# Down stage of a streaming encoder step: ScalarE's norm work of a finished chunk moved later in its order

## The chip, the cores and the metric

The kernel runs on one core of a Trainium2 chip. The metric is the device time of one execution in microseconds. Before the change the median of three runs is 1325.32 us (1324.27 to 1325.89).

## The reference

One layer of a hybrid encoder on 1024 prompt frames and 64 sample frames (1088 tokens, width 1024, all fp32):

```
h = modulate(rmsnorm(x)); mix of retention and window attention; x = x + g1 * (mix @ w_out)
h2 = modulate(rmsnorm(x))
a, b = split(h2 @ w_up);  y = (silu(causal_conv(a)) * b) @ w_down        # D_FF = 2816
x = x + g2 * y
out = rmsnorm(x) * (1 + scale_f) + shift_f                                # final norm, adaLN
```

scale_f and shift_f come from silu(c) @ w_ada_f + b_ada_f. The change touches the last three lines alone: the down projection and the final norm.

## The kernel before, in words

Everything is transposed: features lie on partitions, tokens along the free axis. fp32 products are made from two parts: each weight tile is split into a rounded high half (ScalarE, a copy to fp32r) and the rest (GpSimd, a subtraction), and each output takes three matmuls (high x high, high x low, low x high).

The down stage runs 3 token chunks (364, 362, 362 tokens) x 22 row tiles of w_down = 66 steps, numbered q = 22 c + f with q from 0 to 65. A step multiplies one 128-row tile of the weights with the matching tile of u for eight output tiles o, each with its own PSUM bank: 24 matmuls. Each chunk reads all 22 weight tiles again.

- SP's queue (from L692) issues, at its index q, u tile q + 6 (load_u, L655) and weight tile q + 6 (load_down, L646). Weight tiles land in a ring of three raw buffers, so load q waits until GpSimd has split tile q - 3. The u tiles have a ring of eight, so u tile q waits until TensorE has ended step q - 8. In the same order stand the residual tiles of x (L676), the 16 loads of the last modulation weights (load_last_ada, L678, each waiting for VectorE's dots two tiles earlier) and the stores of finished chunks (store_y, L683).
- ScalarE (from L1171) at index q makes the high half of weight tile q (down_hi, L1092) and writes it into a ring of ten split tiles (w_more 4, w_hl 3, w_extra 3). Between the splits stand, written out by hand, the work of the chunk that is done: eight squares (final_square, L1142), the root of the mean (final_root, L1151) and eight modulations (final_modulate, L1157).
- GpSimd (down_lo, L1312) makes the low halves in order.
- VectorE: the dots of the last modulation weights, tiles 0 to 8 (last_ada_dots, L1832: two halves each, prompt and sample), then for each chunk eight evictions with the residual added (down_out, L1807), eight norm adds (final_add, L1817: a copy and seven adds into acc), the reciprocal (L1845); for chunk 0 dots 9 to 15; then eight scalings (final_scale, L1847).
- TensorE (from L2235): in the first four steps of chunks 1 and 2 it leaves out output tile 7, as bank 7 holds the norm's sum over partitions (final_sum, L2206), which it multiplies after step f = 2; after f = 3 it waits for the root and makes tile 7 of the four steps. The last four steps of chunk 2 run output tile by output tile.

ScalarE's squares use a ring of two buffers, so a square waits for VectorE's add two squares earlier, and the first of them waits for the first eviction. The order of every engine is fixed in the text: an engine that waits for one instruction holds all behind it.

Of the kernel before, what the change touches and what calls it, by code (L numbers as in the profile page):

```python
# [37 lines left out]
FT = D_FF // P  # L38
# [40 lines left out]
            [(CHUNKS[i][0], sum(CHUNKS[i])) for i in c]] + [(k, 0, T) for k in range(2, KT - 1)]  # L79
           + [(KT - 1, a, a + n) for a, n in CHUNKS])  # L80
LATE = 4

OUT_JOBS = ([(o, n) for o in range(1, 8) for n in (0, 1)] + [(o, n) for o in (4, 5, 3, 7) for n in (2, 3)]
            + [(o, n) for n in (2, 3) for o in (6, 1, 2)])
# [27 lines left out]
def hymba_step(nc, x_t, w_units, w_ada, b_ada, cond, gains, conv_wb, conv_st, sinks, ck_t, cv_in, st_in,  # L112
# [4 lines left out]
    with ExitStack() as ctx:  # L117
# [254 lines left out]
        def pieces(c):  # L372

            a, n = CHUNKS[c]
            if c < 2:
                return [(0, a, n, 0)]
            return [(0, a, C2P, 0), (C2P, S_PROMPT, S_SAMPLE, 1)]
# [118 lines left out]
        def _(sp):  # L496
# [149 lines left out]
            def load_down(q):  # L646
                c, f = divmod(q, FT)
                if q < 3:
                    sp.wait_ge(bl_ready, PRODUCTS * FT)
                else:  # L650
                    sp.wait_ge(dl_ready, q - 3 + 1)
                sp.dma_start(w_raw[:, q % 3], w_units[down_unit(f)].rearrange("p (k m) -> p k m", k=KT)).then_inc(
                    dw_loaded[q % 3], 16)

            def load_u(q):  # L655
                c, f = divmod(q, FT)
                a, n = CHUNKS[c]
                if q < U_RING:
                    sp.wait_ge(product, 2 * PRODUCTS * FT - PRODUCTS)
                else:  # L660
                    sp.wait_ge(down_step, q - U_RING + 1)
                if c == 0:
                    sp.wait_ge(u_hi_stored, 16 * (f + 1))
                    sp.wait_ge(u_lo_stored, 16 * (f + 1))
                sp.dma_start(u_hl[:, q % U_RING, :, 0:n].bitcast(F32), u_dram[f, :, :, a:a + n].rearrange("w p t -> p w t")).then_inc(
                    du_loaded[q % U_RING], 16)

            def load_residual(c):
                a, n = CHUNKS[c]
                sp.wait_ge(x1_stored[0], 32)  # L670
                sp.wait_ge(x1_stored[1], 80)
                sp.wait_ge(x1_stored[2], 32)
                sp.wait_ge(product, 2 * PRODUCTS * FT)
                sp.wait_ge(u_ready, FT)
                sp.wait_ge(ext_ready, FT)
                sp.dma_start(x_res[:, :, a:a + n], x1_dram[:, :, a:a + n]).then_inc(x1_again[c], 16)  # L676

            def load_last_ada(t):  # L678
                if t >= 2:
                    sp.wait_ge(ada_d_used, 2 * (t - 2) + 2)  # L680
                sp.dma_start(ada_d[:, t % 2], w_ada[48 + t]).then_inc(ada_d_loaded[t % 2], 16)

            def store_y(c, k0, k1, by_act, by_dve):  # L683
                a, n = CHUNKS[c]
                sp.wait_ge(y_by_act, by_act)
                if by_dve:
                    sp.wait_ge(y_seq, by_dve)
                sp.dma_start(y_v[:, k0:k1, a:a + n], x_res[:, k0:k1, a:a + n]).then_inc(stored, 16)
# [10 lines left out]
            for q in range(3 * FT):  # L699
                c, f = divmod(q, FT)  # L700
                if q == 1:
                    sp.dma_start(silu_d[:, :, :], cond.partition_broadcast(P)).then_inc(cond_again, 16)
                if 2 <= q < 34 and q % 2 == 0:
                    load_last_ada((q - 2) // 2)
                if q + 6 < 3 * FT:
                    load_u(q + 6)
                    load_down(q + 6)
                if q in (8, 26, 46):
                    load_residual(c)
                if c == 1 and f == 20 or c == 2 and f == 12:  # L710
                    store_y(c - 1, 0, 4, 8 * c - 4, 0)
                    store_y(c - 1, 4, 8, 8 * c, 0)
            store_y(2, 0, 2, 19, 0)
            store_y(2, 5, 6, 19, 2)
            store_y(2, 2, 5, 21, 2)
# [6 lines left out]
        def _(act):  # L722
# [357 lines left out]
            def silu(f):  # L1080
                act.wait_ge(conv_seq, 3 * f + 3)
                act.activation(conv[:, :], conv[:, :], ACT.Silu).then_inc(silu_ready, 1)

            def u_hi(f):

                act.wait_ge(u_ready, f + 1)
                if f > 0:
                    act.wait_ge(u_hi_stored, 16 * f)
                    act.wait_ge(u_lo_made, f)
                act.activation(acc[:, :].bitcast(F32R), up_b[f % 2][:, :], ACT.Copy).then_inc(u_hi_made, 1)  # L1090

            def down_hi(q):  # L1092

                act.wait_ge(dw_loaded[q % 3], 16 * (q // 3 + 1))
                if q < W_MORE:
                    act.wait_ge(product, 2 * PRODUCTS * FT - PRODUCTS)
                elif q < W_RING:
                    act.wait_ge(product, 2 * PRODUCTS * FT)
                    if q >= W_MORE + 3:
                        act.wait_ge(u_lo_stored, 16 * FT)  # L1100
                else:
                    act.wait_ge(down_step, q - W_RING + 1)
                act.activation(w_down(q)[:, 0], w_raw[:, q % 3], ACT.Copy).then_inc(dh_ready, 1)  # L1103
# [38 lines left out]
            def final_square(c, k):  # L1142

                a, n = CHUNKS[c]
                item = 8 * c + k
                act.wait_ge(down_evac, item + 1)
                if item >= 2:
                    act.wait_ge(fsq_used, item - 1)
                act.activation(sq[:, k % 2, 0:n], x_res[:, k, a:a + n], ACT.Square).then_inc(fsq_ready, 1)

            def final_root(c):  # L1151
                n = CHUNKS[c][1]
                act.wait_ge(fsum_ready, c + 1)
                act.activation(std[:, c, 0:n], bank[7 if c < 2 else 0][:, 0:n], ACT.Sqrt, bias=eps_sb[:, 0:1],
                               scale=1.0 / D).then_inc(fstd_ready, 1)

            def final_modulate(c, k):  # L1157

                if c == 2 and k in FINAL_POOL:
                    act.wait_ge(scaled_pool, FINAL_POOL.index(k) + 1)  # L1160
                elif c == 2:
                    act.wait_ge(scaled_dve, 17 + k - len(FINAL_POOL))
                else:
                    act.wait_ge(scaled_dve, 8 * c + k + 1)
                for o, tok, m, part in pieces(c):
                    y = x_res[:, k, tok:tok + m]
                    ins = act.activation(y, y, ACT.Identity, bias=mod[:, 48 + 2 * k + 1, part:part + 1],
                                         scale=scale_n[:, 2, k, part:part + 1])
                ins.then_inc(y_by_act, 1)

            for q in range(3 * FT):  # L1171
                c, f = divmod(q, FT)
                if q > 2:
                    down_hi(q)
                if q == 3:
                    silu(FT - 1)
                    u_hi(FT - 1)
                if q == 6:
                    act.wait_ge(cond_again, 16)
                    act.activation(silu_d[:, :, :], silu_d[:, :, :], ACT.Silu).then_inc(silu_d_ready, 1)  # L1180
                if c > 0:
                    if f < 2:
                        for k in range(4 * f, 4 * f + 4):
                            final_square(c - 1, k)
                    if f == 3:
                        final_root(c - 1)
                    if c == 1 and 15 <= f < 19 or c == 2 and 5 <= f < 9:
                        for k in (0, 1):
                            final_modulate(c - 1, 2 * (f - (15 if c == 1 else 5)) + k)
            for k in range(8):  # L1190
                final_square(2, k)
            final_root(2)
# [708 lines left out]
        def _(pe):  # L1901
# [333 lines left out]
            for c in range(3):  # L2235
                for f in range(FT):
                    q = FT * c + f
                    if c == 0 or f >= LATE:
                        if c == 2 and f >= FT - LATE:
                            continue  # L2240
# [8 lines left out]
                    down_tiles(q, range(7), False)  # L2249
                    if f == LATE - 2:  # L2250
                        pe.wait_ge(down_evac, 8 * c)
                        final_sum(c - 1)
                    if f == LATE - 1:
                        pe.wait_ge(fstd_ready, c)
                        for late in range(LATE):
                            down_tiles(FT * c + late, (7,), True).then_inc(down_step, 1)
            for o in range(8):
                for f in range(FT - LATE, FT):
                    down_tiles(2 * FT + f, (o,), False)
# [135 lines left out]
```

## Time and profile before

| | us |
|---|---|
| median of three runs | 1325.32 |
| the profiled execution, its own time | 1324.34 |
| its span, first to last instruction | 1322.5 |
| TensorE busy | 1254.9 |
| VectorE busy | 840.2 |
| ScalarE busy | 517.5 |
| GpSimd busy | 520.5 |

The down stage begins at 1030.3 us of the span. A row of a timeline gives the start, the duration, the engine and line, the operation, tiles out and in, how many like instructions are merged in it, and in square brackets how long the engine was idle before it and what it waited for. Matmuls of TensorE are pipelined, so its busy time is not time at its peak.

### The profile page before, as it was taken

What the parts mean: (1) busy time and instruction counts of PE and PEld (TensorE: products, weight loads), DVE (VectorE), ACT (ScalarE), POOL (GpSimd) and SP (SyncE); (2) the same over time, 40 slices, a digit from 0 to 9 for tenths busy, and PEclk for the clock granted to TensorE, in tenths of its full rate; (3) what the DMA queues carried; (4) which work ended last, traced back from release to release, by engine and by line L of the source; (5) the groups of instructions that cost most, each with busy time, mean ns of one, the idle gap of its engine ahead of it and who ended that gap; (6) DMA issues with size and microseconds to landing.
All of it is one profiled execution on the core that took longest, in us unless ns stands there. A gap on an engine that the chain in (4) does not pass through costs nothing.

```text
span 1322.5 us, 22445 instructions
## 1 busy us (share of the span) xinstructions
PE 1254.9 (95%) x8537; PEld 1182.0 (89%) x8537; DVE 840.2 (64%) x1503; ACT 517.5 (39%) x1029; POOL 520.5 (39%) x313
## 2 busy tenths in 40 slices
PE   5999999999999999779999999999999999999995
PEld 3568988988989899779999999999999999999995
DVE  6988477396496637995666666666665468663305
ACT  4454345344345513543333333433333323333422
POOL 0012131031232514544353534435352577775760
PEclk9999999999999899899999999999999999999998
DMA  9413032222233412103223232222322898686971
GB/s 363 177 58 125 25 121 79 81 80 87 74 112 103 149 60 99 58 32 132 99 100 115 92 124 99 100 99 100 115 94 83 324 367 289 238 310 213 332 258 46
DMA packets 74392, 185.55 MB, mean 140 GB/s; under 512 B 7424, under 2 KB 39744, under 8 KB 74048
## 3 DMA queue, kind: packets, MB, share of 16 engines
q1 hardware_dynamic: 72640, 183.63, 38.9%
q8 instruction: 59, 0.97, 0.3%
q10 hardware_dynamic: 1664, 0.72, 0.2%
q14 instruction: 29, 0.24, 0.1%
HBM read 150.14 MB, written 34.19 MB: 139 GB/s over the span
## 4 chain that ended last, share of the span: by engine, by line
PE 68%; DVE 12%; POOL 6%; issue 5%; DMA 5%; ACT 2%; SPq 1%; DVEq 0%; ACTq 0%; POOLq 0%
PE bank L2189 33%; PE bank L1922 14%; PE bank L2229 9%; PE bank L2165 5%; DMA w_raw<-in_w_units 3%; POOL w_extra L1315 2%; POOL w_more L1315 2%; PE bank L2036 2%; DVE std L1559 1%; PE bank L2006 1%; PE bank L2021 1%; DVE ada_out L1352 1%; DVE act_hl L1406 1%; POOL w_hl L1315 1%; POOL w_hl L1276 1%
## 5 line engine op out<-in xcount | busy, mean ns | idle before, releaser
L1922 PE MATMUL bank<-act_hl,w_hl 128*128 128x362 f32 (+1 forms) x1368 | 256.5, 336 | 1.3 <-DVE act_hl L1406 1.3
L1922 PEld LDWEIGHTS bank<-act_hl,w_hl 128*128 128x128 f32 x1368 | 223.3, 188 | 10.6 <-issue 8.3
L1203 POOL TENSOR_TENSOR w_hl<-w_raw,w_hl 128x1024 fp32r<-128x1024 f32 x21 | 51.3, 2444 | 332.5 <-ACT w_hl L730 332.5
L2229 PE MATMUL bank<-u_hl,w_more 128*128 128x362 f32 (+1 forms) x672 | 116.3, 332 | 2.6 <-POOL w_more L1315 2.3
L2189 PE MATMUL bank<-x_blocks_a,w_hl 128*128 128x272 f32 x864 | 114.0, 291 | 4.9 <-issue 4.9
L2229 PEld LDWEIGHTS bank<-u_hl,w_more 128*128 128x128 f32 x672 | 113.5, 191 | 3.3 <-POOL w_more L1315 2.6
L2189 PEld LDWEIGHTS bank<-x_blocks_a,w_hl 128*128 128x128 f32 x864 | 111.6, 191 | 5.3 <-issue 5.1
L2189 PE MATMUL bank<-x_blocks_a,w_ext 128*128 128x272 f32 x840 | 110.1, 290 | 4.3 <-DVE prod_sb L1664 2.4
L2189 PE MATMUL bank<-x_blocks_b,w_hl 128*128 128x272 f32 x864 | 112.7, 288 | 1.6 <-ACT x_blocks_b L1013 1.3
L2189 PEld LDWEIGHTS bank<-x_blocks_b,w_hl 128*128 128x128 f32 x864 | 109.8, 188 | 2.4 <-DVE up_b L1669 1.3
L2189 PEld LDWEIGHTS bank<-x_blocks_a,w_ext 128*128 128x128 f32 x840 | 107.5, 190 | 5.0 <-issue 2.6
L2189 PE MATMUL bank<-x_blocks_b,w_ext 128*128 128x272 f32 x840 | 108.3, 287 | 0.0
L2189 PEld LDWEIGHTS bank<-x_blocks_b,w_ext 128*128 128x128 f32 x840 | 106.2, 188 | 0.0
L1315 POOL TENSOR_TENSOR w_more<-w_raw,w_more 128x1024 fp32r<-128x1024 f32 x28 | 76.0, 2734 | 49.6 <-ACT w_more L1103 49.6
L2229 PE MATMUL bank<-u_hl,w_hl 128*128 128x362 f32 (+1 forms) x480 | 83.6, 330 | 3.1 <-POOL w_hl L1315 2.8
L1276 POOL TENSOR_TENSOR w_ext<-w_raw,w_ext 128x512 fp32r<-128x512 f32 x40 | 52.9, 1340 | 83.2 <-ACT w_ext L990 83.2
L1276 POOL TENSOR_TENSOR w_hl<-w_raw,w_hl 128x512 fp32r<-128x512 f32 x40 | 52.3, 1323 | 81.2 <-ACT w_hl L990 81.2
L2229 PEld LDWEIGHTS bank<-u_hl,w_hl 128*128 128x128 f32 x480 | 80.1, 189 | 4.3 <-POOL w_hl L1315 3.4
L2229 PE MATMUL bank<-u_hl,w_extra 128*128 128x362 f32 (+1 forms) x432 | 74.0, 330 | 1.9 <-POOL w_extra L1315 1.9
L2229 PEld LDWEIGHTS bank<-u_hl,w_extra 128*128 128x128 f32 x432 | 72.0, 188 | 3.0 <-POOL w_extra L1315 2.8
L1315 POOL TENSOR_TENSOR w_hl<-w_raw,w_hl 128x1024 fp32r<-128x1024 f32 x20 | 52.8, 2654 | 33.6 <-ACT w_hl L1103 33.6
L2165 PE MATMUL bank<-act_hl,w_hl 128*128 128x272 f32 x480 | 64.1, 297 | 2.0 <-POOL w_hl L1269 2.0
(233 smaller groups left out, 2277.7 us busy)
## 6 DMA issues: line engine op xcount, KB each, us to landing
w_raw<-in_w_units SPq DMA_DIRECT2D x139, 512.0 KB, 4.5
ada_w<-in_w_ada_t SPq DMA_DIRECT2D x36, 512.0 KB, 3.6
u_hl<-u_dram SPq DMA_DIRECT2D x44, 362.0 KB, 5.5
u_dram<-acc SPq DMA_DIRECT2D x22, 544.0 KB, 2.7
u_dram<-up_b SPq DMA_DIRECT2D x22, 544.0 KB, 2.7
ada_d<-in_w_ada_t SPq DMA_DIRECT2D x16, 512.0 KB, 5.7
u_hl<-u_dram SPq DMA_DIRECT2D x22, 364.0 KB, 7.3
xm<-in_x_t SPq DMA_DIRECT2D x2, 1448.0 KB, 13.8
```

Source lines behind the costliest of these rows:

```text
L1203: pool.tensor_tensor(w_hl[:, slot, 1], w_raw[:, slot], w_hl[:, slot, 0].bitcast(F32), ALU.subtract).then_inc(wl_ready, 1)
L1276: pool.tensor_tensor(w_block(q)[:, 1], a_source(f, i), w_block(q)[:, 0].bitcast(F32), ALU.subtract).then_inc(bl_ready, 1)
L1315: pool.tensor_tensor(w_down(q)[:, 1], w_raw[:, q % 3], w_down(q)[:, 0].bitcast(F32), ALU.subtract).then_inc(dl_ready, 1)
L1352: dve.tensor_tensor_reduce(out, ada_place[place], silu_c[:, s], 1.0, 0.0, ALU.mult, ALU.add, mod_part[:, part, s:s + 1]).then_inc(ada_used, 1)
L1406: dve.tensor_tensor(act_hl[:, 1, k, :], xm[:, k, :], act_hl[:, 0, k, :].bitcast(F32), ALU.subtract).then_inc(lo_ready, 1)
L1559: dve.reciprocal(std[:, c, 0:n], std[:, c, 0:n]).then_inc(inv_ready, 1)
L1922: ins = pe.matmul(bank[c][:, 0:m], w_hl[:, slot, w, k, :], act_hl[:, x, k, a:a + m], start=(pas == 0 and i == 0), stop=(pas == 2 and i == ...
L2006: ins = pe.matmul(bank[3 + g][0:n, 0:kn], aq[h, t:t + n], ak[h, kb[0][0]:kb[0][0] + kn], start=True, stop=True)
L2036: ins = pe.matmul(bank[6][h, 0:n], av_tok[0:k[1], k[3], h], prob_t[0:k[1], r, g, i, 0:n], start=(i == 0), stop=(i == len(kb) - 1))
L2165: ins = pe.matmul(bank[r % 3][:, 0:HC], w_of[:, w, k, :], act_hl[:, x, k, HC * n:HC * n + HC], start=(pas == i == 0), stop=(pas == 2 and i ...
L2189: ins = pe.matmul(n[:, 0:HC], w_block(q)[:, w, P * k:P * (k + 1)], x_half(h)[:, i, x, k, :], start=(first and pas == k == 0), stop=(pas == ...
L2229: ins = pe.matmul(bank[o][:, 0:m], w_down(q)[:, w, o, :], u_hl[:, q % U_RING, x, 0:m], start=(f == pas == 0), stop=(f == FT - 1 and pas == 2))
```

## The change

ScalarE: at its indices 22 and 23 (44 and 45 for the second boundary) stood four squares each, at 25 (47) the root, at 37 to 40 the modulation of chunk 0 and at 49 to 52 that of chunk 1. Now all eight squares and the root stand at index 29 (51), behind weight split 29 (51), and the modulations at 46 to 49 and 60 to 63. SP: the stores of chunk 0 and 1 stand at index 48 and 62 (42 and 56 before), and modulation loads 11 to 15, which stood at 24, 26, 28, 30 and 32, at 28, 30, 32, 34 and 36.

```
+FINAL_AT = (46, 60)
+STORE_AT = (48, 62)
@@ block.sync
-                if 2 <= q < 34 and q % 2 == 0:
+                if 2 <= q < 24 and q % 2 == 0:
                     load_last_ada((q - 2) // 2)
+                if 28 <= q < 38 and q % 2 == 0:
+                    load_last_ada(11 + (q - 28) // 2)
...
-                if c == 1 and f == 20 or c == 2 and f == 12:
-                    store_y(c - 1, 0, 4, 8 * c - 4, 0)
-                    store_y(c - 1, 4, 8, 8 * c, 0)
+                if q in STORE_AT:
+                    done = STORE_AT.index(q)
+                    store_y(done, 0, 4, 8 * done + 4, 0)
+                    store_y(done, 4, 8, 8 * done + 8, 0)
@@ block.scalar
-                if c > 0:
-                    if f < 2:
-                        for k in range(4 * f, 4 * f + 4):
-                            final_square(c - 1, k)
-                    if f == 3:
-                        final_root(c - 1)
-                    if c == 1 and 15 <= f < 19 or c == 2 and 5 <= f < 9:
+                for done in range(2):
+                    step = q - FT * (done + 1)
+                    if step == 7:
+                        for k in range(8):
+                            final_square(done, k)
+                        final_root(done)
+                    if FINAL_AT[done] <= q < FINAL_AT[done] + 4:
                         for k in (0, 1):
-                            final_modulate(c - 1, 2 * (f - (15 if c == 1 else 5)) + k)
+                            final_modulate(done, 2 * (q - FINAL_AT[done]) + k)
```

## Rows read from the trace of the kernel before

**Rows 1.** The page, part 1: busy us, share of the span, instructions.

```profile
PE 1254.9 (95%) x8537; PEld 1182.0 (89%) x8537; DVE 840.2 (64%) x1503; ACT 517.5 (39%) x1029; POOL 520.5 (39%) x313
```

**Rows 2.** Timeline of TensorE, first chunk boundary: start, us, line, tiles, count, [idle before].

```profile
1119.66 3.71 PE L2229 MATMUL bank<-u_hl,w_more 128*128 128x362 f32 x21 [0.30 <-PE bank L2229]
1125.65 5.28 PE L2229 MATMUL bank<-u_hl,w_more 128*128 128x362 f32 x21 [2.29 <-POOL w_more L1315]
1130.77 3.68 PE L2229 MATMUL bank<-u_hl,w_hl 128*128 128x362 f32 x21
1134.29 0.77 PE L2210 MATMUL bank<-acc,ones 128*128 128x364 f32 x2
```

**Rows 3.** Windows, TensorE: stretch, busy (count), granted clock, DMA share, GB/s.

```profile
1126.00:1131.00 5.00, 5.00 (x23) 0.66 0.53 182
```

**Rows 4.** Timeline of TensorE, middle of chunk 1 to the second boundary.

```profile
1189.63 8.21 PE L2229 MATMUL bank<-u_hl,w_extra 128*128 128x362 f32 x48 [1.19 <-POOL w_extra L1315]
1197.68 16.22 PE L2229 MATMUL bank<-u_hl,w_more 128*128 128x362 f32 x96
1214.20 3.71 PE L2229 MATMUL bank<-u_hl,w_hl 128*128 128x362 f32 x21 [0.30 <-DVE x_res L1813]
1219.47 3.76 PE L2229 MATMUL bank<-u_hl,w_hl 128*128 128x362 f32 x21 [1.56 <-POOL w_hl L1315]
1224.49 3.79 PE L2229 MATMUL bank<-u_hl,w_hl 128*128 128x362 f32 x21 [1.26 <-POOL w_hl L1315]
1228.12 0.77 PE L2210 MATMUL bank<-acc,ones 128*128 128x362 f32 x2
```

**Rows 5.** Timeline of ScalarE, first boundary and the modulation of chunk 0.

```profile
1109.38 1.06 ACT L1103 ACTIVATE w_more<-w_raw 128x1024 fp32r<-128x1024 f32 x1 [3.31 <-DMA w_raw<-in_w_units]
1117.23 1.01 ACT L1149 ACTIVATE sq<-x_res 128x364 f32<-128x364 f32 x2 [6.78 <-DVE x_res L1813]
...
1129.15 1.28 ACT L1154 ACT_TABLE_LOAD   x1
...
1184.24 1.27 ACT L1167 ACTIVATE x_res<-x_res,mod,scale_n 128x364 f32<-128x364 f32 x2 [7.51 <-DVE x_res L1852]
```

**Rows 6.** Timeline of GpSimd, first boundary.

```profile
1107.60 6.72 POOL L1315 TENSOR_TENSOR w_more<-w_raw,w_more 128x1024 fp32r<-128x1024 f32 x2
1123.26 2.34 POOL L1315 TENSOR_TENSOR w_more<-w_raw,w_more 128x1024 fp32r<-128x1024 f32 x1 [8.93 <-ACT w_more L1103]
```

**Rows 7.** Timeline of VectorE, first boundary.

```profile
1108.77 3.30 DVE L1839 CUSTOM_DVE_ANT_0 ada_d<-ada_d,silu_d 128x1024 f32<-128x1024 f32 x1
...
1113.65 1.76 DVE L1839 CUSTOM_DVE_ANT_0 ada_d_out<-ada_d,silu_d 128x1024 bf16<-128x1024 f32 x1 [1.57 <-DMA ada_d<-in_w_ada_t]
...
1115.45 1.23 DVE L1839 CUSTOM_DVE_ANT_0 ada_d<-ada_d,silu_d 128x1024 f32<-128x1024 f32 x1
...
1116.61 4.12 DVE L1813 SCALAR_TENSOR_TENSOR x_res<-bank,mod,x_res 128x364 f32<-128x364 f32 x8
1120.64 0.34 DVE L1826 COPY acc<-sq 128x364 f32<-128x364 f32 x1
1121.08 1.82 DVE L1829 TENSOR_TENSOR acc<-acc,sq 128x364 f32<-128x364 f32 x3
1123.60 2.39 DVE L1829 TENSOR_TENSOR acc<-acc,sq 128x364 f32<-128x364 f32 x1 [0.70 <-ACT sq L1149]
```

**Rows 8.** One line's instructions (output stage eviction, L1723): duration ns min/median/max.

```profile
L1723 DVE SCALAR_TENSOR_TENSOR xm<-bank,mod,xm x35: 270/490/503, 456.1 to 548.4; 128x272 f32<-128x272 f32 x21, 128x208 f32<-128x208 f32 x7, 128x64 f32<-128x64 f32 x7
```

**Rows 9.** Timeline of SP's queue, DMA issues around the first boundary.

```profile
1114.35 0.33 SPq L652 DMA_DIRECT2D w_raw<-in_w_units  x1
...
1144.65 0.46 SPq L652 DMA_DIRECT2D w_raw<-in_w_units  x1
```

**Rows 10.** Line L652 (weight loads of the down stage), from issue to landing.

```profile
DMA to landing us min/median/max: 3.4/4.8/10.3
```

**Rows 11.** Windows, all engines, ahead of the first boundary: last DMA share, GB/s.

```profile
1107.00:1114.00 7.00, 7.00 (x44) 7.00 (x43) 5.29 (x5) 1.06 (x1) 7.00 (x3) 1.00 1.00 374
```

## The prediction

> **What bounds the kernel now.** I first read the busy table of the page: TensorE is busy 95% of the span, ScalarE and GpSimd 39% each [rows 1]. So the end is set by TensorE, and only what makes TensorE wait counts. Next the timeline of TensorE in the down stage, where the edit lies (from 1030.3 us). One step there (one row tile of the down weights times one chunk of u) is 24 matmuls and takes 4.0 us; a step with seven of eight output tiles takes 3.52 us (1134.29 less 1130.77) [rows 2]. The reader is to look for the brackets, which are TensorE's idle time. Behind the first chunk boundary it waits 2.29 us for a weight split of GpSimd, and the 21 matmuls that follow take 5.28 us where their neighbours take 3.71: the granted clock is 0.66 of full in 1126 to 1131 [rows 2, 3]. This is the lower of the two levels (1.2 GHz) for part of the stretch, it cost 5.28 - 3.71 = 1.57 us, and it came after that idle time. At 1189.63 it waits 1.19 us, and behind the second boundary 1.56 and 1.26 us, again for GpSimd, without slow matmuls [rows 4]. Together 2.29 + 1.57 + 1.19 + 1.56 + 1.26 = 7.87 us: all that the change can win.
>
> Then ScalarE's and GpSimd's timelines tell why. ScalarE finishes the high half of weight tile 22 at 1110.44, and next in its order stand squares 0 to 3 of chunk 0, whose input comes only when TensorE ends step 21; it sits 6.78 us for them [rows 5]. GpSimd, which ends split 22 at 1107.60 + 6.72 = 1114.32, has nothing for 8.93 us [rows 6]. The 1.19 us has the same form: ScalarE stood 7.51 us at step 37's modulation, waiting for VectorE's scaling, which stands behind the last modulation dots [rows 5].
>
> **The change part by part.** Nothing is added in number: 16 squares, two roots and 16 modulations of chunks 0 and 1, four stores and five loads of modulation weights (tiles 11 to 15) are moved. I walk the three stalls.
>
> *First boundary.* Squares and root now stand behind weight split 29. So ScalarE goes on to splits 23, 24, 25 and the 2.29 us and 1.57 us go. What is late next? TensorE needs the sum of squares after the seven-tile part of step 24, in its own order (L2250), at 1119.66 + 3 x 3.52 = 1130.2 [rows 2]. When are the squares summed now? They wait for split 29, whose load is issued when GpSimd has done split 26 (the raw ring holds three tiles) and TensorE step 21, behind load 28. The chain:
> GpSimd's split takes 2.4 us alone and 3.4 us while VectorE's dots run (6.72 us for two) [rows 6]; VectorE's dot half takes 1.23 us alone and 3.30 us beside a split [rows 7]. The last pair of dots before the boundary starts at 1113.65, so splits 23 and 24 are of the long kind: 1117.7, 1121.2. Splits 25 and 26 follow at 2.4: 1123.6, 1126.0. Load 29 then leaves at once, as load 25 left at 1114.35 behind split 22 [rows 9]. A weight load takes 3.4 us at least, 4.8 in the median [rows 10]; I take 4.2, between the two: the stretch before ran the DMA engines full (share 1.00, 374 GB/s [rows 11]) and this one carries five weight tiles, four of u and two of modulation weights. It lands at 1130.2. Split 29 on ScalarE, 1.06 us [rows 5]: 1131.3. GpSimd then holds split 29, from about 1131.6, to 1134.0.
> Now VectorE's adds. An add of the norm takes 0.54 us, and three in a row step by (1.82 - 0.54) / 2 = 0.64 us; but the one that started beside a split took 2.39 us, to the end of that split [rows 7]. So the copy (0.34 us) or the first add ends with split 29, and seven adds follow: 1134.1 + 6 x 0.64 + 0.54 = 1138.5. (If the copy slips through, 1137.9; the trace has no copy beside a split, and I take the locked value, as for the add.)
> The Trainium skill, page "SBUF — State Buffer", section "Who interferes with whom", says that a VectorE instruction with two SBUF inputs, or one in a two-port mode such as a copy, and a GpSimd instruction exclude each other for the whole instruction. The trace agrees for the add. By the rule the copy is locked too: 1138.5, and its other half, that an instruction with one SBUF input is free, would leave the evictions unlocked.
> So the sum of squares starts at 1138.5 where it started at 1134.29: TensorE idles 8.3 us in one piece instead of 2.29 in a smaller one, and comes out 4.2 us later. The clock's fall comes on top, since the 1.57 us of before lie ahead of 1134.29; I take 1.6 us. Result +5.8 us. Bounds: with loads at 3.4 us the sum comes at 1136.5, +2.2, and the clock between 0 and 2: +2.2 at least. With a load of 6 us (towards the 10.3 maximum [rows 10]) 1140.3 and 2 us of clock: +8.0.
>
> Free of charge, with their cover: VectorE's eight evictions (4.12 us [rows 7]) come some 2 us later, as GpSimd now holds the dots up; TensorE's wait for the sum hides that. Evictions read one SBUF and one PSUM input; a like one in the output stage takes 0.50 us at most in 35 [rows 8]. The table load (1.28 us [rows 5]) falls into ScalarE's wait for the sum. Splits 30 on now stand behind the root: load 30 waits in any case for TensorE's step 22, whose last tile comes after step 25 (about 1144), while step 30 is due near 1162; before, load 30 left at 1144.65 [rows 9]. On SP's queue, modulation load 11 stood before u tile 30 and waited for VectorE's dot 9; it is now four steps later and waits for nothing. That gain hides behind the same 18 us of lead.
>
> *The 1.19 us.* Modulation of chunk 0 moves from step 37 to 46. The last dots move by four steps of 4 us, from about 1183 to about 1200, and chunk 0's scaling by as much; ScalarE is at step 46 near 1208. The wait of 7.51 us goes and TensorE gets 1.19 us back (0 if ScalarE meets VectorE still at it). VectorE must be free at the boundary at 1213.9, 14 us of cover.
>
> *Second boundary.* I count from the end of step 43, 1197.68 + 16.22 = 1213.90; the sum started at 1228.12, 14.22 later [rows 4]. Now no dots run, so the weights are as far ahead as the u ring lets them. u tile 51 waits for the end of step 43, then weight 51 leaves at +0.5 and lands at +4.6 (3.4 to 4.8 us [rows 10]), is split at +5.7; GpSimd ends at +8.1; adds end at +8.2 + 4.4 = +12.6. TensorE is there at 0.30 + 3 x 3.52 = +10.86. It waits 1.7 us in one piece, and comes out 1.6 us earlier than before. Does the clock fall? 1.56 us of idle time did not bring it down, 2.29 did [rows 2, 4]; 1.7 is nearer to the first, so no. Bounds: -2.8 (two stalls gone, no wait), and +1.1 (load 51 late by 1 us, clock down).
>
> The stores: chunk 0's stands behind u tile 54, chunk 1's at step 62, behind the last weight load, and about seven steps ahead of the end; 1.5 MB each are through by then. The last chunk's tail is untouched. Chunk 2's burst of loads after the late tiles has 16 us of lead, so 0; if that cover is gone, 1 to 2 us.
>
> Sum: +5.8 - 1.2 - 1.6 = +3.0 us. On the profiled execution's own time, 1324.34, this is 1327.3; the median of the runs shown is 1.0 above that, 1325.32, and I state the forecast against it: **1328.3 us**.
>
> **The rivals.**
> (a) The squares come in time and the stalls just vanish. For it: the three stalls are named as ScalarE's waits, and ScalarE has 61% of the span free [rows 1]. It needs the sum at 1130.2, so load 29 landed by 1122, four us before GpSimd could have done split 26 even at 2.4 us each. Full gain 7.87: 1317.5; half of it, if the sum is there by 1134: 1321. Chance 0.17. This is the case on the faster side.
> (b) The chain is the one above, but at its quick end: loads at 3.4 us, copy not locked, the clock back at once. Then +2.2 to +3.5 - 1.2 - 2.0, within 0.2% of before: 1325.3. Chance 0.3.
> (c) Clock falls at both boundaries, or the late burst of loads starves step 30 on: +5.8 - 1.2 + 1.1 or more, 1331 to 1334. For it: 1.7 us against 2.29 is no wide margin. Chance 0.13.
> Forecast: the remaining 0.4, 1326.5 to 1330.5.
>
> **How the numbers follow.** A measurement of this kernel tells about 0.2% (2.65 us) from no change. Slower by more holds (c), and 0.34 of the forecast's 0.4: 0.47. Within: (b) and the forecast's other 0.06: 0.36. Faster: (a), 0.17. The range leaves out (a)'s far end and (c)'s: 1322.5 to 1332.
>
> **What would show it.** TensorE's timeline: no bracket before step 23, but one of 7 to 9 us, released by VectorE's add, before the first sum (L2210), and a short one before the second; granted clock below 1 after the first. ScalarE: splits 23 to 29 unbroken, then eight squares, starting near 1131; the 7.51 us wait gone. VectorE: a copy or add of over 1.5 us beside split 29. SP: weight load 29 at about 1126. I am wrong if split 29 is done by 1127, if the sum starts before 1135, or if chunk 1 shows a stall that I have at nothing.

## The result and the profile after

The change makes the kernel slower. Median of five runs 1333.88 us (1330.62 to 1335.3) against 1325.89 (1324.27 to 1327.3) for the kernel before in five runs: ratio 1.0058, 95% interval 1.0042 to 1.0074, some 8 us. The change is 0.6%, and the interval lies clear of no change. The direction was forecast, the size was not: 3.0 us forecast, and the range ended at 1332.0. In the second group of experiments below one execution of the kernel before took 3123.69 us; the ratios leave it out, and without it that group's median is 1325.69 instead of 1325.93.

TensorE is as busy as before [rows 1] in a longer span. The page, part 1:

```profile
PE 1254.1 (94%) x8537; PEld 1182.6 (89%) x8537; DVE 842.8 (63%) x1503; ACT 519.6 (39%) x1029; POOL 523.3 (39%) x313
```

The profiled execution takes 1333.75 us with a span of 1331.9. Its step 20 begins 2.39 us later than in the profiled execution of before (1113.62 against 1111.23), ahead of the first instruction that the change moves in time, so this part is the difference of two executions (in the seven experiments step 20 begins at 1111.5 to 1113.7, and their text is that of the changed or the old kernel up to there). I count from step 20 on. TensorE's timeline, first boundary, to be read beside [rows 2]:

```profile
1113.62 8.13 PE L2234 MATMUL bank<-u_hl,w_more 128*128 128x364 f32 x48
1122.58 7.20 PE L2234 MATMUL bank<-u_hl,w_more 128*128 128x362 f32 x42 [0.83 <-DVE x_res L1818]
1129.62 3.67 PE L2234 MATMUL bank<-u_hl,w_hl 128*128 128x362 f32 x21
1143.90 1.55 PE L2215 MATMUL bank<-acc,ones 128*128 128x364 f32 x2 [10.61 <-DVE acc L1834]
1144.71 5.95 PE L2234 MATMUL bank<-u_hl,w_hl 128*128 128x362 f32 x21
...
1168.46 16.11 PE L2234 MATMUL bank<-u_hl,w_more 128*128 128x362 f32 x96
```

The wait of 2.29 us before step 23 is gone, and one of 10.61 us stands before the sum of squares. Step 25, right behind it, takes 5.95 us where the like one before took 3.94; here are that step and step 30 in the kernel before:

```profile
1134.62 3.94 PE L2229 MATMUL bank<-u_hl,w_hl 128*128 128x362 f32 x21
...
1156.37 16.11 PE L2229 MATMUL bank<-u_hl,w_more 128*128 128x362 f32 x96
```

The granted clock, windows of TensorE (stretch, busy, clock, DMA share, GB/s):

```profile
1137.00:1143.50 6.50, 0.00 (x0) 0.50 0.00 0
1144.00:1149.00 5.00, 5.00 (x15) 0.50 0.00 0
1149.00:1155.00 6.00, 6.00 (x38) 0.99 0.45 149
```

So TensorE worked at 1.2 GHz for some 5 us behind the idle time. The second boundary, beside [rows 4]:

```profile
1208.31 16.22 PE L2234 MATMUL bank<-u_hl,w_more 128*128 128x362 f32 x96
1224.86 10.77 PE L2234 MATMUL bank<-u_hl,w_hl 128*128 128x362 f32 x63 [0.33 <-DVE x_res L1818]
1237.36 0.85 PE L2215 MATMUL bank<-acc,ones 128*128 128x362 f32 x2 [1.73 <-DVE acc L1834]
```

Where the time went (starts taken from these rows and from the rows of before):

| stretch | before | after | difference | forecast |
|---|---|---|---|---|
| step 20 to first sum | 23.06 | 30.28 | +7.22 | +4.2 |
| first sum to step 30 | 22.08 | 24.56 | +2.48 | +1.6 |
| step 30 to step 44 | 57.83 | 56.40 | -1.43 | -1.2 |
| step 44 to second sum | 13.92 | 12.50 | -1.42 | -1.6 |
| second sum to the end | 94.4 | 94.5 | +0.1 | 0 |
| together | | | +7.0 | +3.0 |

The chain into the first sum, on the other engines. SP's queue (weight loads 27, 28, 29), then how long the weight loads of 1117 to 1136 took to land (KB each, median us), then all engines' windows of 1117 to 1126, whose last two numbers are DMA share and GB/s:

```profile
1124.19 0.33 SPq L654 DMA_DIRECT2D w_raw<-in_w_units  x1
...
1126.56 0.33 SPq L654 DMA_DIRECT2D w_raw<-in_w_units  x1
...
1129.15 0.33 SPq L654 DMA_DIRECT2D w_raw<-in_w_units  x1
```

```profile
w_raw<-in_w_units SPq DMA_DIRECT2D x5, 512.0 KB, 6.0
```

```profile
1117.00:1126.00 9.00, 8.17 (x50) 7.84 (x49) 8.72 (x12) 2.56 (x4) 7.67 (x4) 1.00 1.00 358
```

ScalarE (L1108 are splits, 28 and 29 here; L1154 squares, L1159 the root), beside [rows 5]:

```profile
1133.28 1.06 ACT L1108 ACTIVATE w_extra<-w_raw 128x1024 fp32r<-128x1024 f32 x1 [3.60 <-DMA w_raw<-in_w_units]
1135.48 1.06 ACT L1108 ACTIVATE w_extra<-w_raw 128x1024 fp32r<-128x1024 f32 x1 [1.14 <-DMA w_raw<-in_w_units]
1136.44 0.89 ACT L1154 ACTIVATE sq<-x_res 128x364 f32<-128x364 f32 x2
1139.35 3.72 ACT L1154 ACTIVATE sq<-x_res 128x364 f32<-128x364 f32 x6 [2.02 <-DVE acc L1831]
1143.09 1.28 ACT L1159 ACT_TABLE_LOAD   x1
1145.48 0.57 ACT L1159 ACTIVATE std<-bank,eps_sb 128x364 f32<-128x364 f32 x1 [1.11 <-PE bank L2215]
```

GpSimd, splits 28 and 29, then VectorE, beside [rows 6, 7]:

```profile
1134.41 4.65 POOL L1320 TENSOR_TENSOR w_extra<-w_raw,w_extra 128x1024 fp32r<-128x1024 f32 x2 [2.26 <-ACT w_extra L1108]
```

```profile
1117.21 3.44 DVE L1844 CUSTOM_DVE_ANT_0 ada_d_out<-ada_d,silu_d 128x1024 bf16<-128x1024 f32 x1 [2.26 <-DMA ada_d<-in_w_ada_t]
...
1121.84 4.12 DVE L1818 SCALAR_TENSOR_TENSOR x_res<-bank,mod,x_res 128x364 f32<-128x364 f32 x8
1136.96 2.30 DVE L1831 COPY acc<-sq 128x364 f32<-128x364 f32 x1 [11.00 <-ACT sq L1154]
1139.36 4.39 DVE L1834 TENSOR_TENSOR acc<-acc,sq 128x364 f32<-128x364 f32 x7
```

The evictions were done at 1125.96, and VectorE then had nothing for 11.00 us: the input of the squares was there, ScalarE stood at the loads of weights 27 to 29. Weight 29 left at 1129.15 and ScalarE could take it at 1135.48, 6.33 us later. The copy of 0.34 us [rows 7] then took 2.30, to the end of GpSimd's split 29 at 1139.06, and seven adds followed in 4.39.

### The profile page after: what moved, and what is told of

Read it like the earlier page. It is cut to its first block, busy times and chain, and to the rows that moved or that the text cites. A ratio compares the mean times of both kernels' runs of the same rounds, so it can differ in the third digit from the quotient of the medians.

```text
span 1331.9 us, 22445 instructions
## 1 busy us (share of the span) xinstructions
PE 1254.1 (94%) x8537; PEld 1182.6 (89%) x8537; DVE 842.8 (63%) x1503; ACT 519.6 (39%) x1029; POOL 523.3 (39%) x313
## 4 chain that ended last, share of the span: by engine, by line
PE 71%; DVE 10%; POOL 5%; issue 5%; DMA 4%; ACT 2%; SPq 2%; DVEq 0%; ACTq 0%; PEldq 0%; POOLq 0%
PE bank L2194 32%; PE bank L1927 14%; PE bank L2234 12%; PE bank L2170 5%; DMA w_raw<-in_w_units 4%; PE bank L2041 2%; POOL w_more L1320 1%; POOL w_extra L1320 1%; DVE std L1564 1%; PE bank L2011 1%; PE bank L2026 1%; DVE ada_out L1357 1%; POOL w_hl L1281 1%; PE bank L2075 1%; PE bank L2078 1%
## 5 line engine op out<-in xcount | busy, mean ns | idle before, releaser
L1208 POOL TENSOR_TENSOR w_hl<-w_raw,w_hl 128x1024 fp32r<-128x1024 f32 x21 | 53.7, 2558 | 329.7 <-ACT w_hl L735 329.7
L1844 DVE CUSTOM_DVE_ANT_0 ada_d_out<-ada_d,silu_d 128x1024 bf16<-128x1024 f32 x16 | 39.2, 2452 | 51.3 <-DMA ada_d<-in_w_ada_t 51.1
```

Source lines behind the costliest of these rows:

```text
L1208: pool.tensor_tensor(w_hl[:, slot, 1], w_raw[:, slot], w_hl[:, slot, 0].bitcast(F32), ALU.subtract).then_inc(wl_ready, 1)
L1844: dve.tensor_tensor_reduce(out, ada_d[:, t % 2], silu_d[:, s], 1.0, 0.0, ALU.mult, ALU.add, mod_part_d[:, t, s:s + 1]).then_inc(ada_d_used, 1)
```

## The experiments

Seven kernels, 6 to 12 executions each, in two groups that ran each on one chip (e1, e3, e4; e2b, x1, x2, x3); the median of before is 1325.54 us beside the first three and 1325.93 beside the other four. "First boundary" is the time from the start of step 20 to the sum of squares in the profiled execution, "second" from step 44 to its sum (before 23.06 and 13.92, changed kernel 30.28 and 12.50).

| kernel | median us | ratio to before | first | second |
|---|---|---|---|---|
| e1, modulation, stores, loads only | 1324.59 | 0.9987 (0.9979 to 0.9996) | 23.71 | 13.92 |
| e2b, squares moved | 1334.61 | 1.0071 (1.0054 to 1.0088) | 29.11 | 14.48 |
| e3, squares ahead of split 29 | 1326.70 | 1.0005 (0.9995 to 1.0014) | 27.35 | 10.56 |
| e4, two loads later | 1331.58 | 1.0042 (1.0028 to 1.0056) | 28.30 | 14.25 |
| x1, squares at 25 and 47 | 1318.68 | 0.9952 (0.9936 to 0.9967) | 18.94 | 10.58 |
| x2, squares at 25 and 49 | 1317.46 | 0.9938 (0.9925 to 0.9951) | 19.60 | 10.56 |
| x3, squares at 27 and 49 | 1321.43 | 0.9966 (0.9952 to 0.9979) | 22.56 | 10.58 |

### e1: all but the squares

```
-                    if step == 7:
-                        for k in range(8):
+                    if step in (0, 1):
+                        for k in range(4 * step, 4 * step + 4):
                             final_square(done, k)
+                    if step == 3:
                         final_root(done)
```

> The squares and the root stand at their old places (ScalarE's indices 22, 23, 25 and 44, 45, 47); modulations, stores and modulation loads 11 to 15 as in the changed kernel. Theory (the squares' place is the whole loss): both boundaries look as before (TensorE waits of about 2.3, and 1.6 + 1.3 us; first boundary from the start of step 20 to the sum near 23.1 us, where the changed kernel has 30.3), and only the 1.19 us wait near the middle of chunk 1 goes: 1.0 to 1.4 us below the kernel before. Rival (the later modulations, stores and loads carry part of the loss, by the burst of loads after the late tiles or by VectorE's dots being pushed): 2 us or more above the kernel before.

Measured 0.95 us below before, at the small end of the forecast; the interval (up to 0.9996) just excludes that nothing changed. The first boundary has its old wait:

```profile
1127.37 5.08 PE L2235 MATMUL bank<-u_hl,w_more 128*128 128x362 f32 x21 [2.92 <-POOL w_more L1321]
```

and TensorE runs from step 30 (1158.10) to 1214.2 without a wait, so the 1.19 us of [rows 4] are gone; the second boundary takes 13.92 us, as before. So the later modulations, stores and loads win about one microsecond and cost nothing that shows. The rival falls.

### e2b: the squares alone

From the kernel before, with squares and root at index 29 and 51; chunk 1's modulation had to follow its squares and stands at 60, its store at 62. (e2, which left them at 49 and 56, has no time: ScalarE would wait at index 49 for scalings that need the squares and the root of its own index 51, and the kernel never ends.)

```
-                    if f < 2:
-                        for k in range(4 * f, 4 * f + 4):
+                    if f == 7:
+                        for k in range(8):
                             final_square(c - 1, k)
-                    if f == 3:
                         final_root(c - 1)
...
```

> Squares and roots at ScalarE's indices 29 and 51 as in the changed kernel; chunk 0's modulation and store at 37 and 42 and the modulation loads as before; chunk 1's modulation and store at 60 and 62, since they must follow the squares. Theory: first boundary 30 us from the start of step 20 to the sum (23.1 before), 2.5 us of lower clock behind it, second boundary 12.5 (13.9 before). Chunk 0's modulation at index 37 waits for VectorE's dots 9 to 15, which now start 10 us later, so the 1.2 us wait near step 38 stays: 8 to 10 us above the kernel before. Rival: the loss needs the later loads of modulation weights; then no more than 4 us above.

Measured 8.7 us above before, where the changed kernel is 8.0 above, and the intervals overlap: the squares' place is the whole loss. TensorE at steps 22 and 23 and at both sums, and ScalarE at the modulation of chunk 0:

```profile
1122.22 8.69 PE L2228 MATMUL bank<-u_hl,w_more 128*128 128x362 f32 x42 [2.55 <-DVE x_res L1812]
...
1140.65 1.55 PE L2209 MATMUL bank<-acc,ones 128*128 128x364 f32 x2 [6.25 <-DVE acc L1828]
...
1236.11 1.54 PE L2209 MATMUL bank<-acc,ones 128*128 128x362 f32 x2 [3.74 <-DVE acc L1828]
```

```profile
1187.75 1.27 ACT L1167 ACTIVATE x_res<-x_res,mod,scale_n 128x364 f32<-128x364 f32 x2 [7.31 <-DVE x_res L1851]
```

The first boundary is 29.11 us, a little under the 30 expected, and is made up otherwise than in the changed kernel: TensorE first waits 2.55 us for an eviction, the 42 matmuls behind that take 8.69 us instead of 7.20 (granted clock 0.57 in 1122 to 1126), and only 6.25 us are left to wait for the sum. The sum comes when ScalarE and VectorE have it ready, so what TensorE loses ahead of it adds nothing.

Two parts of the expectation missed. ScalarE's wait at index 37 is 7.31 us, as expected, but TensorE does not feel it: ScalarE comes out of it 3.5 us later than before (1187.75 against 1184.24), while TensorE reaches step 37 8.9 us later (1193.18 against 1184.29). And the second boundary is slower than before, not faster: its wait is 3.74 us, and the sum's two matmuls take 1.54 us, the length that they have at the first sum of the changed kernel under a clock of 0.50.

### e3: squares ahead of split 29

```
             for q in range(3 * FT):
                 c, f = divmod(q, FT)
+                for done in range(2):
+                    if q - FT * (done + 1) == 7:
+                        for k in range(8):
+                            final_square(done, k)
                 if q > 2:
                     down_hi(q)
...
                     if step == 7:
-                        for k in range(8):
-                            final_square(done, k)
                         final_root(done)
```

> As the changed kernel, but squares stand ahead of weight split 29 (51) instead of behind it, the root stays behind. Theory (the sum is late because the squares wait for a weight load that lands 6 us after its issue): the first square starts right behind split 28, about 1.2 to 2.2 us earlier than in the changed kernel, GpSimd holds only split 28, and the wait before the first sum shrinks from 10.6 to 8 to 9 us; at the second boundary squares follow split 50 and start with the evictions, so the wait of 1.7 us there is gone: 3 to 5 us below the changed kernel, still above the kernel before. Rival (VectorE's adds, held by GpSimd's splits, are the long part): no more than 1 us below the changed kernel, as the copy and adds then meet splits 28 and 29 both.

TensorE at both sums, then VectorE's copy and adds:

```profile
1138.96 1.55 PE L2217 MATMUL bank<-acc,ones 128*128 128x364 f32 x2 [7.67 <-DVE acc L1836]
```

```profile
1230.56 0.77 PE L2217 MATMUL bank<-acc,ones 128*128 128x362 f32 x2
```

```profile
1132.12 2.20 DVE L1833 COPY acc<-sq 128x364 f32<-128x364 f32 x1 [8.13 <-ACT sq L1154]
1134.42 4.39 DVE L1836 TENSOR_TENSOR acc<-acc,sq 128x364 f32<-128x364 f32 x7
```

The first boundary is 2.93 us shorter than in the changed kernel (the wait 7.67, a little under the 8 to 9 expected) and the second 1.94, without a wait. That is 4.9 us, at the top of the 3 to 5 forecast. The medians differ by 7.2; so do the two profiled executions (span 1331.9 and 1324.9), and there 2.0 of it lies ahead of step 20. Against the kernel before, e3 was expected to stay above it; the ratio, 1.0005, is no different from 1. The copy starts 20.51 us behind step 20 instead of 23.34 and is held here too (2.20 us), by split 28. So the gain at the first boundary is that the squares no longer wait for the last load, with the hold as long as before, and the rival falls. What the hold costs by itself, at most the 2 us by which the copy is longer than 0.34, e3 does not test.

### e4: two modulation loads out of the burst

```
-                if 2 <= q < 24 and q % 2 == 0:
+                if 2 <= q < 20 and q % 2 == 0:
                     load_last_ada((q - 2) // 2)
-                if 28 <= q < 38 and q % 2 == 0:
-                    load_last_ada(11 + (q - 28) // 2)
+                if 25 <= q < 32:
+                    load_last_ada(9 + q - 25)
```

> As the changed kernel, but modulation loads 9 and 10 (0.5 MB each), which SP issues at its indices 20 and 22 between the weight loads that split 29 waits for, go to indices 25 and 26, the others follow to 31. Theory (weight loads 27 to 29 land late, 6.3 to 6.7 us after issue where I had taken 4.2, as the DMA engines are full): loads land 1 to 2 us sooner, split 29 starts 2 to 3 us sooner counted from the start of step 20, and the sum too: 2 to 3 us below the changed kernel. Rival (the delay is in GpSimd's splits and not in the loads): within 0.5 us of the changed kernel at the boundary.

TensorE at both sums; then issue to landing of the weight loads of 1110 to 1160 us, which is 4.4/6.0/9.1 in the changed kernel:

```profile
1141.81 1.55 PE L2215 MATMUL bank<-acc,ones 128*128 128x364 f32 x2 [8.55 <-DVE acc L1834]
```

```profile
1237.74 1.54 PE L2215 MATMUL bank<-acc,ones 128*128 128x362 f32 x2 [3.52 <-DVE acc L1834]
```

```profile
DMA to landing us min/median/max: 3.4/4.5/9.4
```

The loads land sooner: weight 29 takes 4.50 us from issue to split (1128.88 to 1133.38) where it took 6.33, split 29 starts 19.9 us behind step 20 instead of 21.9, and the sum comes 1.98 us sooner, at the low end of the 2 to 3 forecast. The rival falls. It is not the DMA share that tells the two kernels apart: while load 29 is under way it is as high in e4 (share and GB/s last), and 0.93 and 0.96 in the same four microseconds of the changed kernel:

```profile
1128.00:1130.00 2.00, 2.00 (x14) 2.00 (x13) 0.00 (x0) 0.60 (x1) 2.00 (x2) 1.00 1.00 366
1130.00:1132.00 2.00, 2.00 (x14) 2.00 (x13) 0.00 (x0) 0.84 (x1) 1.21 (x1) 1.00 0.86 318
```

What differs is how much is queued: the changed kernel has modulation tiles issued at 1117.61 and 1124.57, among weight loads 26 to 28, and e4 has not. The medians differ by 2.3, and their intervals overlap. The profiled execution of e4 is the slowest of its eleven (1336.62 us, 5.0 above the median), so what it shows beyond the first boundary may not be typical: the second boundary is 1.7 us longer than in the changed kernel, and the clock falls there as well (the sum takes 1.54 us instead of 0.77, step 47 6.14 instead of 3.95). VectorE's scaling of chunk 0 runs beside GpSimd's splits for

```profile
1197.29 19.08 DVE L1857 TENSOR_TENSOR x_res<-x_res,std 128x364 f32<-128x364 f32 x8
```

where the changed kernel took 12.44 us and the kernel before 3.67. Whether that makes weight 51 late (5.6 us from issue to split, 3.9 in the changed kernel) was not tested; in e2b it takes 5.9 us though the scaling was over long before.

### x1, x2, x3: where the squares should stand

```
+SQUARES_AT = (25, 47)        # x1;  (25, 49) x2;  (27, 49) x3
...
-                    if step == 7:
+                    if q == SQUARES_AT[done]:
```

> As the changed kernel, but squares and root together behind weight split 25 and 47, three steps behind the boundary instead of seven. Theory: the squares wait only for the evictions, the sum is there by 131 us on a scale where TensorE comes to it at 133 (first boundary 19 to 20.5 us from step 20 to the sum, no wait there and no fall of the clock), splits 26 on start right behind the root and are in time by 1 us; second boundary 10.9 us: 6 to 8 us below the kernel before. Rival: ScalarE, which now waits for the root with only splits to 25 (47) made, starves TensorE at step 26 (48): 1 to 3 us of that are lost again, 3 to 5 us below the kernel before.

> As x1, the second boundary's squares and root behind split 49 instead of 47. Theory: in chunk 1 the weights are as far ahead as the ring of u lets them, so ScalarE stands at index 49 before the boundary either way: within 1 us of x1. Rival (starving at step 48 in x1): 1 to 2 us below x1.

> As x2, the first boundary's squares and root behind split 27 instead of 25. Theory: split 27 is at 1128.6 us on the changed kernel's scale, GpSimd holds it to 1132, the adds end at 1136.6 and TensorE is there at 1133: a wait of 3 to 4 us and a fall of the clock of about 1.5 us, 4 to 6 us above x2. Rival (a later place costs only where ScalarE waits for a load of over 6 us, as at 29): within 1.5 us of x2.

TensorE in x1 and x3 at the first sum:

```profile
1131.79 0.77 PE L2216 MATMUL bank<-acc,ones 128*128 128x364 f32 x2
```

```profile
1135.87 0.85 PE L2216 MATMUL bank<-acc,ones 128*128 128x364 f32 x2 [2.78 <-DVE acc L1835]
```

and x2, TensorE at both boundaries, then ScalarE at the first:

```profile
1122.71 7.22 PE L2235 MATMUL bank<-u_hl,w_more 128*128 128x362 f32 x42 [0.91 <-DVE x_res L1819]
1129.77 3.66 PE L2235 MATMUL bank<-u_hl,w_hl 128*128 128x362 f32 x21
1133.27 0.77 PE L2216 MATMUL bank<-acc,ones 128*128 128x364 f32 x2
...
1211.72 10.72 PE L2235 MATMUL bank<-u_hl,w_hl 128*128 128x362 f32 x63 [0.30 <-PE bank L2235]
1222.28 0.77 PE L2216 MATMUL bank<-acc,ones 128*128 128x362 f32 x2
```

```profile
1122.60 1.01 ACT L1155 ACTIVATE sq<-x_res 128x364 f32<-128x364 f32 x2
1126.95 3.72 ACT L1155 ACTIVATE sq<-x_res 128x364 f32<-128x364 f32 x6 [3.34 <-DVE acc L1832]
...
1134.08 0.57 ACT L1160 ACTIVATE std<-bank,eps_sb 128x364 f32<-128x364 f32 x1 [2.10 <-PE bank L2216]
1134.54 1.05 ACT L1109 ACTIVATE w_hl<-w_raw 128x1024 fp32r<-128x1024 f32 x1
```

x2 takes 1317.46 us, 8.5 below the kernel before and 16 below the changed one. At both boundaries TensorE now waits for neither weights nor sum; what is left is 0.91 us for an eviction at the first. x1 is 7.3 below before. In x2 ScalarE stands at the root until 1134.65 and makes split 26 right behind it, in x1 likewise; TensorE shows no wait for it in either, so the rival of x1 falls. The median of x2 is 1.2 below that of x1, which is in the range of x2's rival (1 to 2); their intervals overlap, and the traces decide: the second boundary is 10.58 us in x1 and 10.56 in x2, and x1 has no wait at step 48. x3 pays 2.78 us at the first sum and is 4.0 above x2, at the low end of the forecast (4 to 6), so its rival falls too; its step 25 takes 3.93 us, so the forecast fall of the clock did not come.

## Why the prediction was wrong

The mechanism, the places and all signs were right; two terms of the first boundary were too small, the landing of weight load 29 above all.

- *What bounds, and the three stalls.* Right. e1 shows that the last one goes by the modulation's place (-1.43 in the changed kernel, -1.2 forecast); x1 and x2 show that the other two can be had.
- *"I take 4.2, between the two."* This is the step that failed. Weight load 29 took 6.33 us from issue to split, and load 28 6.72. In the chain from step 20 to the sum, the issue of load 29 came 15.5 us behind step 20 (14.8 forecast, +0.7), split 29 started 6.33 behind that (4.2, +2.1), and the sum 8.42 behind that (8.3, +0.1): the 3.0 us by which 30.28 exceeds the forecast 27.3. I had listed the traffic, five weight tiles, four of u and two of modulation weights, which comes to 5 MB in 15 us, and had the stretch before it at share 1.00. With that much queued, a landing time below the median of the whole stage (4.8) was the wrong size; e4 takes two modulation tiles out of the queue, and load 29 lands in 4.50 and the sum comes 2.0 us sooner.
- *"The clock's fall ... I take 1.6 us."* Mis-sized as well: 2.48 us. The row behind 1.6 was a fall after 2.29 us of idle time; here the idle time was 10.61, and TensorE then ran at 0.50 for 5 us. The upper bound of +8.0 for the boundary was passed (9.7) by these two and the 0.7 together.
- *"With loads at 3.4 us the sum comes at 1136.5."* Wrongly summed: 0.8 us less in the load takes 1138.5 to 1137.7, or 1137.9 to 1137.1 with the copy slipping through, so the least for the boundary was +2.8 and not +2.2. Rival (b), "+2.2 to +3.5", starts from the same slip.
- *The adds and the copy.* Right, with the locked value: the copy took 2.30 us, to the end of split 29. The value was chosen as for the add; the Trainium skill (page "SBUF — State Buffer", section "Who interferes with whom") has the same as a rule, that a copy too can be shut out by a GpSimd instruction, and it is borne out by the changed kernel's copy and by e3's (2.20). Its other half as well: the eight evictions, with one SBUF input, took 4.12 us beside GpSimd's splits as before without them.
- *Dots held up, evictions later.* Right in kind (3.44 us for a dot half beside a split, step 22 waits 0.83 us for an eviction), and hidden behind the wait for the sum as said.
- *"14 us of cover" for VectorE at the second boundary.* Too much, though it cost nothing here. The prediction counted it from the end of the dots; the scaling of chunk 0 behind them took 12.44 us beside GpSimd's splits, and VectorE was free 2.43 us before the first eviction. In x2 the scaling ends at 1210.39, as the evictions begin (1210.31), so that order has no cover left. The scaling in the changed kernel:

```profile
1206.16 12.44 DVE L1857 TENSOR_TENSOR x_res<-x_res,std 128x364 f32<-128x364 f32 x8
```

- *Second boundary.* Right: 12.50 us, a wait of 1.73 (1.7 forecast), no fall of the clock. It was near the edge: waits of 3.52 and 3.74 us in e4 and e2b came with a sum at half speed, 2.78 in x3 without.
- *Stores, tail, burst of loads.* Right, 0.1 us.
- *Rivals.* (a) did not come in this form: it needs load 29 landed 10.8 us behind step 20, and the load was not even issued before 15.5; with the squares behind 25 the full gain does come, 8.5 us. (b) needed loads at 3.4 us and an unlocked copy, and had neither. (c) gave the time that was measured, but by another cause: the clock fell at one boundary only, so that its number fits is luck.

The sums account for 7.0 us of the 8.0 between the medians; the remainder is below what one profiled execution tells. Of the 5.6 us between the forecast 1328.3 and the measured 1333.88, 4.0 are these terms, 0.6 is that the kernel before had a median of 1325.89 beside the changed one instead of 1325.32, and 1.0 stays open.

## What to carry to other kernels

Work of a finished tile that is moved back in an engine's order, so that it does not hold up prefetching, takes on the waits of all that it is moved behind: count the loads which those instructions wait for, and check when its own consumer comes. The best of the places tried (22, 25, 27 and 29) is the one behind the last instruction whose input is there before the work's own input, split 25. And in a chain that catches up, take a transfer's time from rows with as much queued beside it, not from the stage's median.

## What was not expected of the hardware

- Idle time of TensorE of 10.61 us was followed by about 5 us at half clock (2.5 us lost), of 2.29, 2.55 (e2b) and 2.92 us (e1) by slow matmuls worth 1.57, 1.5 and 1.4 us (5.28 and 5.08 against 3.71, 8.69 against 7.20), and of 2.78 us in x3 by none. So length alone does not tell whether the clock falls.
- VectorE's scaling of chunk 0, eight instructions of 0.53 us each by themselves, took 19.08 us (e4) and 12.44 us (changed kernel) beside a steady row of splits, and 3.67 us in the kernel before, where GpSimd was idle for most of it.
- At about the same DMA share (0.93 and 0.96 in 1128 to 1132, against 1.00 and 0.86 in e4), a 512 KB load took 6.33 us with two 512 KB modulation tiles among the loads ahead of it, and 4.50 without them (e4).
